# Attention with two pairs in flight: TensorE's logits of pair t+2 issued before pair t's probabilities times values

## The reference, cut to what matters

```python
qg = q.reshape(T, N_KV_HEADS, N_HEADS // N_KV_HEADS, HEAD_DIM)
logits = jnp.einsum('tngd,tjnd->tngj', qg, k_sel).astype(jnp.float32) * (HEAD_DIM ** -0.5)
bias = rel_bias[t5_bucket(qpos[:, None] - idx)]
...
logits = jnp.where(valid[:, None, None, :], logits + bias.astype(jnp.float32), -jnp.inf)
p = jax.nn.softmax(logits, axis=-1).astype(v_sel.dtype)
o = jnp.einsum('tngj,tjnd->tngd', p, v_sel)
```

## Time and profile before

| | us |
|---|---|
| median of 3 runs | 4667.99 (4666.35 to 4671.93) |
| the profiled execution | 4651.54 |
| its span on the core | 4649.7 |
| TensorE busy in the span | 4149.1 (89%) |
| VectorE busy in the span | 2113.4 (45%) |
| ScalarE busy in the span | 681.1 (15%) |

### The profile page before, as it was taken

One profiled execution on the slowest core, in us unless ns is written; L12 is line 12 of the kernel. 1 busy time (PEld: TensorE's weight loads), 2 busy tenths in 40 slices (PEclk: granted clock), 3 DMA queues, 4 the chain that ended last, 5 costly groups with the idle time before them and its releaser, 6 DMA issues. The chain is left out here.

```text
span 4649.7 us, 48762 instructions
## 1 busy us (share of the span) xinstructions
PE 4149.1 (89%) x17996; PEld 2956.1 (64%) x17996; DVE 2113.4 (45%) x3404; ACT 681.1 (15%) x1279; POOL 180.6 (4%) x205
## 2 busy tenths in 40 slices
PE   7999999969987979979979877899988979999997
PEld 5888776646655645646746645566655668888664
DVE  3232210010037879879879785357861143332001
ACT  2000000011021210201201200135610020000000
POOL 0000000000000100100200201300000000000000
PEclk9999999989957979979979978899997989999998
DMA  4221221123141011011011012310022111111111
GB/s 165 91 91 73 92 109 37 37 96 146 68 82 41 24 48 38 19 52 38 15 56 38 31 37 62 101 64 24 5 82 91 59 50 42 41 46 67 47 37 49
DMA packets 94025, 278.11 MB, mean 60 GB/s; under 512 B 18168, under 2 KB 54272, under 8 KB 80880
## 3 DMA queue, kind: packets, MB, share of 16 engines
q1 hardware_dynamic: 81488, 236.19, 15.0%
q0 software_dynamic: 3200, 21.11, 1.3%
q10 hardware_dynamic: 9216, 19.17, 1.2%
HBM read 228.81 MB, written 47.79 MB: 59 GB/s over the span
## 5 line engine op out<-in xcount | busy, mean ns | idle before, releaser
L450 PE MATMUL f_ps<-f_a,f_w 128*128 128x344 f32 x2112 | 614.5, 454 | 14.9 <-DVE room L642 12.6
L670 PE MATMUL banks<-h,arena 128*128 128x344 f32 x1920 | 566.1, 459 | 38.0 <-DMA arena<-in_w_ssd 38.0
L450 PEld LDWEIGHTS f_ps<-f_a,f_w 128*128 128x128 f32 x2112 | 402.4, 191 | 226.3 <-issue 19.9
L670 PEld LDWEIGHTS banks<-h,arena 128*128 128x128 f32 x1920 | 370.6, 193 | 233.7 <-issue 48.1
L346 PE MATMUL f_ps<-h,f_w 128*128 128x258 f32 x1408 | 326.1, 386 | 25.4 <-DMA f_w<-in_w_f2i 25.0
L346 PE MATMUL f_ps<-room 128*128 128x258 f32 x1408 | 330.0, 395 | 2.3 <-issue 1.8
L346 PE MATMUL f_ps<-h,room 128*128 128x258 f32 x1408 | 320.8, 381 | 1.0 <-DVE f_u L595 1.0
L346 PEld LDWEIGHTS f_ps<-h,f_w 128*128 128x128 f32 x1408 | 269.1, 192 | 75.8 <-DMA f_w<-in_w_f2i 25.6
L346 PEld LDWEIGHTS f_ps<-room 128*128 128x128 f32 x1408 | 276.9, 198 | 45.2 <-issue 2.7
L346 PEld LDWEIGHTS f_ps<-h,room 128*128 128x128 f32 x1408 | 267.6, 190 | 39.9 <-DVE f_u L595 1.4
L634 DVE TENSOR_TENSOR f_smp<-f_ps,ada 128x8 f32<-128x8 f32 x16 | 2.7, 167 | 601.5 <-PE f_ps L450 601.5
(11 more groups left out here) (336 smaller groups left out, 4894.5 us busy)
## 6 DMA issues: line engine op xcount, KB each, us to landing
f_wa<-in_w_ada SPq DMA_DIRECT2D x28, 1024.0 KB, 7.7
f_w<-in_w_f1i SPq DMA_DIRECT2D x22, 1024.0 KB, 4.8
f_w<-in_w_f2i SPq DMA_DIRECT2D x22, 1024.0 KB, 4.9
arena<-in_w_ssd SPq DMA_DIRECT2D x40, 512.0 KB, 3.5
f_w<-in_w_f1o SPq DMA_DIRECT2D x16, 704.0 KB, 4.1
f_w<-in_w_f2o SPq DMA_DIRECT2D x16, 704.0 KB, 4.0
room<-in_x SPq DMA_DIRECT2D x16, 516.0 KB, 7.6
scr_x<-room SPq DMA_DIRECT2D x2, 4128.0 KB, 12.1
```

Of the source, the lines that this page charges most:

```text
L450: m = nc.tensor.matmul(ps[n][:, q, 0:NC], wo[:, hf, k], a[:, hf * OK + k, n * NC:(n + 1) * NC], start=hf == 0 and k == 0, stop=hf == 1 and ...
L670: m = nc.tensor.matmul(ps[q][:, c, 0:NC], slots[:, q, k], rhs[:, k, c * NC:(c + 1) * NC], start=k == 0, stop=k == kt - 1)
```

## The change

On TensorE alone, and in one place: the call that makes the logits of pair t+2 is moved from behind the values of pair t to ahead of them. The turns, the filler and `spread_recip` stay ahead of both. No instruction is added or removed in the mathematics, no semaphore and no buffer is added.

```diff
@@ -1138,10 +1138,10 @@
                     x.then_inc(gmm, 1)
                 elif b >= 1 and isinstance(g, int):
                     spread_recip(b - 1, m)
+                if nxt is not None:
+                    logits(t + 2, nxt[0], m)
                 for i in range(0, len(ps), 2):
                     values(i)
-                if nxt is not None:
-                    logits(t + 2, nxt[0], m)
```

## The result

The changed kernel takes **4745.0 us** (median of 4 runs, 4738.54 to 4747.77) against 4668.05 (4666.35 to 4671.93) before: a ratio of **1.0162 [1.0144, 1.0179]**, 77 us more. The forecast was slower by 51 us, 4719, with a range to 4733. The direction and the mechanism came out; the size was too small and the result lies above the range.

What follows compares the result with a forecast made beforehand. From block 4 on, a circle of handovers between TensorE and VectorE bounds the kernel; with filler, TensorE's own work does. 44.9 - 0.8 + 6.6 = +50.7, say +51 us, on 4667.99 gives 4719; range 4690 to 4733.

Steps and rivals of the forecast that it cites:

- The circle: Pairs 31 to 61: copy, masking, logits of u = 1, values, copy close a loop; 8.46 us in block 7, +44.9 together.
- copy to masking: On VectorE, from one pair's copy to the start of the next masking: 0.20 us a pair.
- masking: On VectorE, from masking u = 0 to the end of u = 1: 3.78 us in block 6, 4.18 in block 7.
- to TensorE: Handover from VectorE's reading of u = 1 to TensorE's start: 0.11 us, taken from the index scoring.
- u = 1 alone: On TensorE, the second logits half by itself costs a whole call: 1.72 us in block 6, 1.93 in block 7.
- values to copy: TensorE's run of values plus a 0.07 us gap to VectorE's copy: 1.38 us in block 4, 2.04 in block 7.
- The halves side by side: Logits halves on TensorE run in parallel when both may start; one alone takes 2.0 us, both 1.99, by the index scoring.
- Pairs with filler: 24 pairs where filler covers the masking and both waits are over in time: 0, give or take 0.1 us a pair.
- The early blocks: Blocks 0 to 3: the last two pairs of each have no filler and pay 1.65 us a block on average, +6.6.
- The last wait: Behind pair 61 no logits are left, so VectorE's last wait of 0.78 us goes: -0.8.
- rival 4: Blocks 4 to 7: TensorE's longer waits drop the clock to 1.2 GHz, about 100 us more, 4819; chance 0.03.

Runs made afterwards that it cites:

- experiment 4: Changed kernel with the logits' half u = 0 also waiting until u = 1 of the pair before has been read: 4748.68 us, 1.0173.
- experiment 6: Kernel before, with the new order only in the 24 pairs with filler and the old order in the 40 others: 4667.76 us, 1.0004.
- experiment 1: Changed kernel with VectorE masking both halves of a pair before the bias and maximum of either: 4671.98 us, 1.0015.
- experiment 2: Kernel before, old order kept, with VectorE masking both halves before the bias and maximum of either: 4657.39 us, 0.9979.
- experiment 3: Changed kernel with an unread 256-column matmul between the two logits halves in loop pairs of blocks 4 to 7: 4726.52 us, 1.0129.
- Experiment 5: Changed kernel with only the logits' half u = 0 ahead of the values and u = 1 back behind them: 4724.68 us, 1.0121.

## Why the prediction was right and wrong

**The circle: right.** Its terms in block 6, from the timeline above: copy to masking 0.28 (forecast 0.20), masking 3.79 (3.78), to TensorE 0.05 (0.11), u = 1 alone 1.70 (1.72), values to copy 1.95 (1.82); sum 7.77 against 7.63. The undisturbed intervals are 6.10, 6.93, 7.77 and 8.60 against 5.96, 6.80, 7.63 and 8.46, so 0.14 too little in each, 4.2 us in 30. The mis-sized terms are the two around the copy. These are every second interval; the others are longer by 0.3 to 0.4 (see below), and the shorter ones ahead of a border between blocks make up for it.

**The halves side by side: right**, by a price taken from another stage. The rule named there (the Trainium skill, TensorEngine Tiling (Array Packing), Key Properties) agrees with experiment 4: 1.78 us for both, 1.77 for one.

**Pairs with filler: right**, 7.73 after, and experiment 6. **The early blocks:** 8.3 against 6.6, near it in part by luck. The two intervals priced at the end of each block cost 5.2 more in all; the one behind them, into the next block, was not priced in blocks 0 to 2 and cost 3.1. In block 0 that interval (pair 7 to 8) fell to a clock of 0.81 (8.24 against 7.31 in experiment 1, where it held): 0.9 of the surplus. The same interval fell in experiment 2 (8.36 at 0.80), with the order of before, so this fall is not shown to come from the change. **The last wait:** the interval from pair 61 to 62 went from 6.88 to 6.03, the -0.8 of the forecast; the next one, 6.25 before and in experiment 3, took 7.87 at a clock of 0.78, which turned the sum to +0.8.

**The step that failed is the dismissal of rival 4**, "in the new circle its share is rather higher, since the halves no longer overlap", with "a clock of 1.00" for the kernel before. The share did rise a little: 7.21 of 7.77 us in the undisturbed interval of block 6 above, and in the kernel before, in two neighbours of the same block:

```profile
3302.56:3314.68 12.12, 10.98 (x102) 7.37 (x100) 10.67 (x19) 8.44 (x16) 0.59 (x2) 1.00 0.00 0
```

The clock fell all the same, in 9 of the 30 intervals from pair 31 to 61. If these nine had been as long as like ones where it held (from the same block, or from experiment 3), they would be about 18 us shorter. With the interval into block 1 and the last one, 18 + 0.9 + 1.6, some 20.5 of the 26 us above the forecast are the clock; experiment 3, which took the falls in blocks 4 to 7 away, came 18.5 lower than the changed kernel (4726.52 against 4745.0), and that with what its added matmul costs. The rest, some 5 us, is mostly the circle's gaps. The rival was also priced as all or nothing, 100 us with a chance of 0.03. The fall in part, priced between, belonged into the range. The sentence that it cites from the Trainium skill (TensorE: Matmul & The Clock Gate, Part 1) says that the throttled state is the default and that activity releases it. The trace agrees as far as it goes: the falls came behind pauses, and in experiment 3, with a matmul in the pause, they stayed away from pair 31 on.

**Left open.** What decides a fall. Experiments 3 and 4 show that filling the pause takes the falls away and lengthening it brings more. In blocks 6 and 7 of the changed kernel each of the six pauses of 0.58 to 0.81 us ahead of u = 1 was followed by a fall, and none of the three of 0.25 to 0.31 was. But the pause's length is not all. In block 5 only one of three pauses of 0.63 to 0.65 was followed by a fall; the kernel before has single pauses of 0.62 us in block 7 (and one of 1.30 before 3382.19) with the clock at 1.00, behind transposes. And the fall in the last interval came behind a pause of 1.68 us ahead of the turns (3473.30), not ahead of u = 1, while experiments 3 and 4 have the same pause (1.68 and 1.67) and no fall there. Experiment 5 has the half-row runs without a pause, at 1.00. Whether the half-row form counts beside the pause was not tried by itself. Every second interval, the first of a turn of the loop, is 0.3 to 0.4 us longer (6.38 beside 6.10 in block 4, 7.33 beside 6.93 in block 5); the trace names TensorE's turns as what VectorE waited for there, and this was not tried either.

## What to carry to other kernels

On an engine that takes its list in order, an instruction moved ahead brings its waits with it, and everything that it was moved past stands behind them: look for what waits on that work, and whether a circle closes. Two instructions that run side by side on parts of TensorE are one price; a wait between them makes it two, and a row of a stage where they run apart can tell it. Where a wait has to stand ahead, free what it waits for first (experiment 1 against the change: 73 us), and price a pause of the engine at the lower clock in part, not only as all or nothing.

## What the hardware showed that was not expected

A pause of 0.75 us on TensorE, behind 2 us of half-row matmuls at 1.00, was followed by a fall to 0.50 (1.2 GHz) within the next microsecond, and the clock was at 0.50 from 3451.50 to 3457.30, with TensorE busy throughout. A matmul that nobody reads, put into the pause, took the falls in blocks 4 to 7 away and made the changed kernel 18.5 us faster. And an order of VectorE's list that was written as a control, both maskings ahead of both biases, took 10 us off the kernel before.
